# Two macaron blocks on one core: all 24 products of the modulation rows inside the FFNs, none in the transitions behind the norms

## Chip, cores and metric

One core of one Trainium2 chip runs the whole program. The metric is device time in microseconds (us) of one execution. Five engines run side by side, each with an instruction queue of its own: TensorE (PE; its weight loads are shown as PEld), VectorE (DVE), ScalarE (ACT), GpSimd (POOL) and SyncE (SP). Here SP does nothing but wait and issue the loads of weights. All arithmetic is float32.

## What is computed

There are two models in one program. The first, `first_block`, is a stack of DEPTH = 2 layers over 256 tokens of 1024 features:

```
for i in range(2):
    x = layer_norm(a*x + 0.5*swiglu(x, w1[i,0], w3[i,0], w2[i,0]))     # FFN 0, then norm 0
    x = layer_norm(a*x + token_mixing(x, w_in[i], ...))                # mix,   then norm 1
    x = layer_norm(a*x + 0.5*swiglu(x, w1[i,1], w3[i,1], w2[i,1]))     # FFN 1, then norm 2
    x = layer_norm(a*x + sigmoid(x @ ple_gate[i]) * (p[i] @ ple_proj[i]))  # ple, then norm 3
```

`swiglu` has a hidden width of 2816. The second model (attention, an FFN, an HGRN layer, an FFN) takes that output and a context of 256 tokens. Each of its layers is modulated: from a conditioning vector `c` (and a second one for the context) come six vectors of 1024 for each layer, `silu(c) @ ada_w[l] + ada_b[l]`, with `ada_w[l]` of 1024 x 6144. These are the modulation rows. They depend on `c` alone, so they can be computed at any time before the second model begins.

## The kernel before

**The modulation rows.** The two matrices `ada_w` are cut into 24 blocks of 1024 x 512 (2 MB each, `ADA_BLOCKS`). For each block there is a **product** and a **turn**. `pe_ada_product` (L2522) multiplies the block by `c_wide`, 8 k-tiles by 4 column groups, 32 matmul calls of 128 x 32 weights on 128 columns; the trace shows two instructions for each, 64 in all. ACT copies the bank to `ada_rows` (L2564). `pe_ada_turn` (L2542) transposes that one 128 x 128 tile on PE, and ACT copies 8 columns of it to `modp` (L2576). The blocks are taken in a fixed order, and nothing reads `modp` before `dve_parameters`, which runs in the down projection of the last FFN of layer 1.

**Where they stand.** Two tables say it. `IN_TRANSITION[l][n]` is the number of products in the transition behind norm n of layer l. `IN_FFN[i]` lists the blocks b (of 11) of the up projection in front of which one product is done in FFN i, in both layers; its turn comes in front of block b + 1 (`ffn_ada`, L2550). An assertion makes the sum 24. All engines and SP follow the same two tables.

**The FFN** (`pe_ffn7`, `act_ffn7`, `dve_ffn7`). The products with w1, w3 and w2 are done by a scheme with seven products of quarters in place of eight. In each of the 11 up blocks PE does seven groups of matmuls (112 instructions of 128 x 128 on 128 columns), DVE makes the sums of weight quarters for the next block (`dve_T`, L716), ACT copies four partial results out of PSUM (L670), DVE combines them (L756), and ACT ends a block with a SiLU (L688). Then come six down blocks in two halves. Two forms of the modulation product exist. In an FFN the block of `ada_w` has a place of its own in SBUF (`home`, the tile `f_ada`). SP issues that load from L405, in its queue right behind the loads of up block b, after waiting until ACT has emptied the bank of the product before it (`ada_used`):

```
if homes[0]:
    eng.wait_ge(ada_used, homes[0])
homes[0] += 1
eng.dma_start(f_ada[:], ...).then_inc(ada_landed, 16)
```

In a transition the block of `ada_w` goes through the ring of RING = 3 weight buffers (L359), in order with all other weights; a ring buffer is given back by the first matmul after its use.

**The transition** (`pe_transition` L1024 and below, `act_transition`) turns the normalized `xtok` (two tiles of 128 tokens) into `xT`. The order on PE is: eight transposes of tile 0 (L442), the first product if there is one, eight transposes of tile 1, then for two products: turn, second product, turn; and at the end a wait for DVE's last share of `xT`. On ACT:

```
act_ln_turn(act, l, n, 0, (0, 1), lambda: act_std(act, 1))
if products:
    act_ada_product(act)
act_ln_turn(act, l, n, 1, (0,))
```

`act_ln_turn` writes `xT` (L979), four instructions for each bank, `act_std` takes the square root of the variance for tile 1 (L963) between them, and DVE writes the last four pieces of `xT` (L999). The next stage starts on PE with transposes of parameter rows in the mix (L442 on `rows`), transposes of `p` in the ple (L442 on `xT`), or up block 0 of an FFN (L439).

Of the kernel before, what the change touches and what calls it, by code (L numbers as in the profile page):

```python
# [124 lines left out]
def two_blocks(nc, a, out):  # L125
    ctx = ExitStack()
    with ctx:
# [201 lines left out]
        def k_rows(w, c0, n):  # L329

            return w.rearrange("(k p) n -> p k n", p=P)[:, :, c0:c0 + n]
# [58 lines left out]
        def first_loads(eng, load, wide, ffn):  # L390
# [4 lines left out]
            def modulation(n):  # L395
                for _ in range(n):
                    l2, c0 = next(ada)
                    wide(a["ada_w_2"][l2], c0, 512)
# [8 lines left out]
            for l in range(DEPTH):  # L407
                ffn(a["ffn_w1"][l, 0], 0, a["ffn_w3"][l, 0], 0, a["ffn_w2"][l, 0], modulation_at_home, IN_FFN[0])
                modulation(IN_TRANSITION[l][0])
                wide(W[l], 1536, 288)  # L410
# [9 lines left out]
                wide(a["w_o"][l], 0, 1024)  # L420
                modulation(IN_TRANSITION[l][1])
                ffn(a["ffn_w1"][l, 1], 0, a["ffn_w3"][l, 1], 0, a["ffn_w2"][l, 1], modulation_at_home, IN_FFN[1])
                modulation(IN_TRANSITION[l][2])
                load((None, 0, k_rows(a["ple_w_proj"][l], 0, 1024)))
                wide(a["ple_w_gate"][l], 0, 1024)
                modulation(IN_TRANSITION[l][3])

# [40 lines left out]
        def pe_turn_x(pe, tts, banks):  # L468

            for tt, src in tts:  # L470
                pe.wait_ge(x_ready, pe.due(x_ready))
                for q in range(2):
                    pe.wait_ge(banks[q].freed, banks[q].next_free())
                    bank = banks[q].free_bank()
                    for k in range(4):
                        kt = 4 * q + k
                        mm = pe.turn(bank[:, k * P:(k + 1) * P], src[:, kt * P:(kt + 1) * P])
                        if k == 3:
                            mm.then_inc(banks[q].filled, 1)
# [480 lines left out]
        def act_std(act, n=2):  # L960
            for _ in range(n):
                act.wait_ge(var_ready, act.due(var_ready))
                act.e.activation(small[:, 3:4], small[:, 2:3], ACT.Sqrt).then_inc(std_ready, act.up(std_ready))  # L963
                act.wait_ge(std_ready, act.sent(std_ready))
# [7 lines left out]
        def act_ln_turn(act, l, n, tt, qs, between=None):  # L972

            for q in qs:
                act.wait_ge(to_act.filled, to_act.next_filled())
                bank = to_act.filled_bank()
                for k in range(4):
                    g, b = ln_gb(l, n, 4 * q + k)
                    ins = act.e.activation(xT[:, 4 * q + k, tt * P:(tt + 1) * P], bank[:, k * P:(k + 1) * P], ACT.Identity,  # L979
                                           scale=g, bias=b)  # L980
                    done = to_act.freed if k == 3 else act_step
                    ins.then_inc(done, act.up(done))
                    act.wait_ge(done, act.sent(done))
                    if between and q == 0 and k == 2:
                        between()
            act.sem_inc(x_turned, act.up(x_turned))
# [19 lines left out]
        def act_transition(act, l, n):  # L1006
# [3 lines left out]
            act_ln_turn(act, l, n, 0, (0, 1), lambda: act_std(act, 1))  # L1010
            products = IN_TRANSITION[l][n]
            if products:
# [11 lines left out]
        def pe_transition(pe, l, n):  # L1024

            pe_turn_x(pe, X2[:1], (to_act, to_act))
            products = IN_TRANSITION[l][n]
            if products:
# [1486 lines left out]
        ln_rows = at(arena_cols - 3 * P, P)  # L2515
        lb_rows = at(arena_cols - 3 * P, P)

        IN_TRANSITION = ((2, 0, 2, 0), (2, 0, 0, 0))
        IN_FFN = ((3, 5, 7, 8, 9), (3, 5, 7, 9))
        assert sum(sum(n) for n in IN_TRANSITION) + DEPTH * sum(len(m) for m in IN_FFN) == ADA_BLOCKS  # L2520

        def pe_ada_product(pe, home=False):  # L2522

            if home:
                pe.wait_ge(ada_landed, pe.due(ada_landed, 16))
                blk = f_ada
            else:
                blk = pe.block()
            pe.wait_ge(to_act.freed, to_act.next_free())
            bank = to_act.free_bank()  # L2530
            for k in range(KT):
                for j in range(4):
                    mm = pe.mm(bank[32 * j:32 * j + 32, 0:P], c_wide[:, k], blk[:, k, j * P:(j + 1) * P],
                               k == 0, k == KT - 1)
                    if k == j == 0 and not home:
                        pe.release(mm)
                    if k == KT - 1 and j == 3:
                        mm.then_inc(to_act.filled, 1)
            if not home:
                pe.used()  # L2540

        def pe_ada_turn(pe):  # L2542

            pe.wait_ge(ada_rows_ready, pe.due(ada_rows_ready))
            pe.wait_ge(to_act.freed, to_act.next_free())
            bank = to_act.free_bank()
            pe.turn(bank[:, 0:P], ada_rows[:, pe.ada % 2]).then_inc(to_act.filled, 1)
            pe.ada += 1

        def ffn_ada(marks, product, turn):  # L2550

            def between(b):
                if b - 1 in marks:
                    turn()
                if b in marks:
                    product()

            return between

        def act_ada_product(act, home=False):  # L2560

            act.wait_ge(to_act.filled, to_act.next_filled())
            bank = to_act.filled_bank()
            act.e.copy(ada_rows[:, act.ada_rows % 2], bank[:, 0:P]).then_inc(to_act.freed, act.up(to_act.freed))  # L2564
            act.wait_ge(to_act.freed, act.sent(to_act.freed))
            act.sem_inc(ada_rows_ready, act.up(ada_rows_ready))
            if home:
                act.sem_inc(ada_used, act.up(ada_used))
            act.ada_rows += 1

        def act_ada_turn(act):

            act.wait_ge(to_act.filled, to_act.next_filled())
            bank = to_act.filled_bank()
            n = act.ada
            ins = act.e.copy(modp[:, 8 * n:8 * n + 8].rearrange("p (j s) -> p j s", s=2),  # L2576
                             bank[:, 0:P].rearrange("p (j m) -> p j m", j=4)[:, :, 0:2])
            ins.then_inc(to_act.freed, act.up(to_act.freed))
            act.wait_ge(to_act.freed, act.sent(to_act.freed))
            act.ada += 1  # L2580
# [1072 lines left out]
        def first_pe(pe):  # L3653
            pe_turn_c(pe)
            pe_turn_x(pe, X2, (to_act, to_act))
            pe.wait_ge(c_cols_ready, pe.due(c_cols_ready))
            ada = [ffn_ada(marks, lambda: pe_ada_product(pe, True), lambda: pe_ada_turn(pe)) for marks in IN_FFN]
            for l in range(DEPTH):
# [13 lines left out]
        def first_act(act):  # L3672
            act_turn_c(act)
            act_turn_x(act, X2)
            act.sem_inc(ffn_x_ready, act.up(ffn_x_ready))
            ada = [ffn_ada(marks, lambda: act_ada_product(act, True), lambda: act_ada_turn(act)) for marks in IN_FFN]
            for l in range(DEPTH):
# [116 lines left out]
```

## Time and profile before

| | |
|---|---|
| median of 3 runs | 3774.65 us (3773.93 to 3776.23) |
| profiled execution: its own time | 3775.99 us |
| its span, first to last instruction | 3774.1 us |
| PE busy | 3379.8 us, 90% of the span |
| mean granted TensorE clock | 0.942 |
| loads of `ada_w` through L405 (FFNs) / L359 (ring) | 18 / 6, 2 MB each |

A time in the trace counts from the start of the span. "Busy" says that an instruction was under way. The granted clock is 1.00 at 2.4 GHz and 0.50 at 1.2 GHz; a value between them is a mean over a stretch with both levels.

### The profile page before, as it was taken

The page shows a single profiled execution, that of the slowest core. Times are in us where ns is not written, and L with a number is a line of the kernel's source. Part 1 is how long each engine was busy: PE and PEld are TensorE (multiplying, and loading weights), DVE is VectorE, ACT ScalarE, POOL GpSimd, SP SyncE. Part 2 cuts the span into 40 slices and gives each one's busy share as a digit, 9 for nine tenths or more (in the row PEclk, how much of TensorE's full clock was granted, in tenths as well). Part 3 has the DMA queues.
Part 4 walks back from the last instruction along what each step waited for, and adds up shares of the span by engine and source line. Part 5 has one row for each costly group of instructions (what it writes and reads, how often), then busy time and mean ns, then how long its engine had stood idle before and what let it go on. Part 6 is the DMA issues. An engine that isn't in the chain of part 4 may idle for free.

```text
span 3774.1 us, 44470 instructions
## 1 busy us (share of the span) xinstructions
PE 3379.8 (90%) x18658; PEld 2445.6 (65%) x18658; DVE 1791.2 (47%) x2674; ACT 637.4 (17%) x1204; POOL 37.9 (1%) x76
## 2 busy tenths in 40 slices
PE   8999978868998999987787997889999999998798
PEld 7986675465996997665554895445444444466597
DVE  5653355564655555255564664455210001268565
ACT  1111112101102102110220211144100001233110
POOL 1000000000000000000000000000000000000000
PEclk9999989888999999998898998989999999998899
DMA  7653301103745754400111653110222212221353
GB/s 256 221 200 113 123 1 67 67 1 106 261 153 195 256 177 155 165 26 23 67 45 45 221 202 128 48 67 1 67 67 67 84 61 73 104 97 45 108 166 112
DMA packets 273943, 419.24 MB, mean 111 GB/s; under 512 B 9784, under 2 KB 147360, under 8 KB 273616
## 3 DMA queue, kind: packets, MB, share of 16 engines
q1 hardware_dynamic: 268192, 399.98, 31.2%
q0 software_dynamic: 5088, 15.28, 1.2%
q8 instruction: 149, 2.44, 0.3%
q10 hardware_dynamic: 464, 1.12, 0.1%
q14 instruction: 50, 0.41, 0.0%
HBM read 415.32 MB, written 1.05 MB: 110 GB/s over the span
## 4 chain that ended last, share of the span: by engine, by line
PE 78%; DVE 16%; ACT 3%; issue 2%; DMA 0%; DVEq 0%; ACTq 0%; SPq 0%; PEldq 0%
PE bank L439 76%; PE bank L442 1%; DVE ctok L1682 1%; DVE arena L1671 1%; DVE arena L2244 1%; ACT xT L2655 1%; DVE arena L3081 1%; DVE arena L3454 1%; DVE arena L716 1%; DVE arena L3059 1%; DVE arena L3375 0%; DVE arena L3489 0%; DVE arena L1682 0%; DMA ring<-in_ffn_w 0%; ACT arena L2957 0%
## 5 line engine op out<-in xcount | busy, mean ns | idle before, releaser
L439 PE MATMUL bank<-xT,ring 128*128 128x128 f32 (+3 forms) x3872 | 888.1, 391 | 16.8 <-ACTq L2663 9.8
L439 PE MATMUL bank<-arena 128*128 128x128 f32 (+7 forms) x5428 | 745.1, 300 | 119.7 <-DVE arena L1565 14.5
L439 PEld LDWEIGHTS bank<-xT,ring 128*128 128x128 f32 (+1 forms) x3872 | 607.7, 193 | 294.5 <-issue 241.7
L439 PEld LDWEIGHTS bank<-arena 128*128 128x128 f32 (+3 forms) x5428 | 658.6, 185 | 187.0 <-DVEq L2008 15.3
L439 PE MATMUL bank<-ring,xT 128*128 128x512 f32 (+2 forms) x1408 | 566.8, 560 | 5.3 <-ACTq L1320 2.7
L439 PE MATMUL bank<-ring,arena 128*128 128x256 f32 (+1 forms) x1584 | 523.8, 487 | 22.6 <-ACTq L2473 11.5
L439 PEld LDWEIGHTS bank<-ring,xT 128*128 128x128 f32 x1408 | 262.5, 192 | 293.0 <-issue 285.0
L439 PEld LDWEIGHTS bank<-ring,arena 128*128 128x128 f32 x1584 | 305.6, 194 | 226.0 <-issue 176.8
L442 PE MATMUL bank<-cst,arena 128*128 128x128 f32 x610 | 106.9, 320 | 123.1 <-DVE arena L1627 15.1
L716 DVE TENSOR_TENSOR arena<-ring,arena 128x1024 f32<-128x1024 f32 (+1 forms) x170 | 202.9, 1193 | 5.9
L439 PE MATMUL bank<-arena,ring 128*128 128x128 f32 x1760 | 205.5, 275 | 0.0
L439 PEld LDWEIGHTS bank<-arena,ring 128*128 128x128 f32 x1760 | 201.0, 192 | 0.0
L756 DVE TENSOR_TENSOR arena<-arena,bank 128x256 f32<-128x256 f32 x165 | 69.5, 421 | 270.4 <-PE bank L439 168.6
L442 PEld LDWEIGHTS bank<-cst,arena 128*128 128x128 f32 x610 | 82.6, 164 | 159.0 <-issue 24.4
L670 ACT COPY arena<-bank 128x256 f32<-128x256 f32 x220 | 82.0, 373 | 562.9 <-PE bank L439 561.9
L856 DVE TENSOR_TENSOR arena<-bank,arena 128x512 f32<-128x512 f32 x22 | 15.2, 691 | 298.2 <-PE bank L439 298.2
L716 DVE TENSOR_TENSOR arena<-ring 128x1024 f32<-128x1024 f32 (+1 forms) x85 | 101.5, 1194 | 90.4 <-PE bank L439 67.6
L439 PE MATMUL bank<-xT,arena 128*128 128x128 f32 x880 | 107.2, 275 | 0.0
L716 DVE TENSOR_TENSOR ring<-ring 128x1024 f32<-128x1024 f32 (+1 forms) x85 | 101.5, 1194 | 2.9
L439 PEld LDWEIGHTS bank<-xT,arena 128*128 128x128 f32 x880 | 102.7, 192 | 0.0
L439 PE MATMUL bank<-ctok,arena 128*128 128x128 f32 x640 | 89.4, 294 | 14.4 <-DVE arena L1671 14.4
L2768 DVE TENSOR_TENSOR arena<-bank,lnp 128x512 f32<-128x512 f32 x20 | 13.8, 692 | 185.8 <-PE bank L439 185.8
(390 smaller groups left out, 2380.3 us busy)
## 6 DMA issues: line engine op xcount, KB each, us to landing
ring<-in_ffn_w SPq DMA_DIRECT2D x88, 1024.0 KB, 8.0
ring<-in_w_in SPq DMA_DIRECT2D x32, 2048.0 KB, 7.7
ring<-in_ffn_w_in SPq DMA_DIRECT2D x44, 1024.0 KB, 7.6
arena<-in_ada_w SPq DMA_DIRECT2D x18, 2048.0 KB, 13.8
ring<-in_ffn_w SPq DMA_DIRECT2D x16, 2048.0 KB, 7.8
ring<-in_hgrn_w_in SPq DMA_DIRECT2D x12, 2048.0 KB, 7.8
ring<-in_ffn_w_out SPq DMA_DIRECT2D x8, 2048.0 KB, 7.8
ring<-in_ffn_w SPq DMA_DIRECT2D x8, 1536.0 KB, 6.6
```

The costliest lines, as they stand in the source:

```text
L439: return self.e.matmul(o, lhsT, rhs, start=start, stop=stop, skip_group_check=True)
L442: return self.e.transpose(o, x, ident[0:n, 0:n])
L670: ins = e.copy(f_s[:, i], bank[:, 0:256])
L716: v.tensor_tensor(out_, a_, b_, ALU.subtract).then_inc(T_sums, dve.up(T_sums))
L756: ins = v.tensor_tensor(out_, kept, c, ALU.add)
L1671: v.tensor_tensor(Am[:, 4 * b:4 * b + 4], AT(b), lvlT[:, l:l + 1].broadcast_to([P, 4, P]), ALU.mult).then_inc(level_masked, dve.up(level_m ...
L1682: ins = v.tensor_tensor(X, bank[:].rearrange("p (h n) -> p h n", h=4), X, ALU.add)
L2244: v.reciprocal(dsq[:], dsq[:]).then_inc(dve_step, dve.up(dve_step))
L2655: ins = act.e.activation(xT[:, kt, s * SEQ:(s + 1) * SEQ], bank[:, j * SEQ:(j + 1) * SEQ], ACT.Identity, scale=Amod[:, l, which, kt, s:s + ...
L3059: ins = v.tensor_reduce(am[:, o + qt:o + qt + 1], bank[:], AX.X, ALU.max)
L3081: ins = v.tensor_scalar(pv, pv, r[:, qt:qt + 1], None, ALU.mult)
L3454: step(v.tensor_tensor(halves(dst, h, not back)[i], halves(src, h, not back)[i], halves(hF[back], h, not back)[i], ALU.mult))
```

## The change

The two tables are rewritten. The three pairs of products in transitions (behind norms 0 and 2 of layer 0 and behind norm 0 of layer 1) go. FFN 0 gains the mark 4 in both layers, FFN 1 the marks 4 and 8. The sum stays 24, the blocks keep their order, and each one from the seventh on is computed earlier or later by some places. SP's loads of these six blocks move with them, from L359 into the ring to L405 into `f_ada`.

```diff
-        IN_TRANSITION = ((2, 0, 2, 0), (2, 0, 0, 0))
-        IN_FFN = ((3, 5, 7, 8, 9), (3, 5, 7, 9))
+        IN_TRANSITION = ((0, 0, 0, 0), (0, 0, 0, 0))
+        IN_FFN = ((3, 4, 5, 7, 8, 9), (3, 4, 5, 7, 8, 9))
```

## Rows read from the trace of the kernel before

**Rows 1.** The page: the chain that ended last, and the loads through L405.

```profile
PE 78%; DVE 16%; ACT 3%; issue 2%; DMA 0%; DVEq 0%; ACTq 0%; SPq 0%; PEldq 0%
...
arena<-in_ada_w SPq DMA_DIRECT2D x18, 2048.0 KB, 13.8
```

**Rows 2.** Waits of PE, 1204 to 1413 us, FFN 0 of layer 1: total, times, longest.

```profile
PE bank L439 <- DVE arena L800: 0.4, 1, 0.4
```

**Rows 3.** Timeline of ACT, FFN 0 of layer 0, ends of blocks: start, duration in us.

```profile
49.08 0.63 ACT L688 ACTIVATE arena<-arena 128x512 f32<-128x512 f32 x1 [1.08 <-DVE arena L756]
61.58 0.63 ACT L688 ACTIVATE arena<-arena 128x512 f32<-128x512 f32 x1 [1.08 <-DVE arena L756]
...
130.57 0.63 ACT L688 ACTIVATE arena<-arena 128x512 f32<-128x512 f32 x1 [1.08 <-DVE arena L756]
...
145.27 0.63 ACT L688 ACTIVATE arena<-arena 128x512 f32<-128x512 f32 x1 [1.07 <-DVE arena L756]
```

**Rows 4.** Timeline there: a load of `ada_w`, and the product on PE that uses it.

```profile
117.06 0.37 SPq L405 DMA_DIRECT2D arena<-in_ada_w  x1
...
129.07 1.96 PE L439 MATMUL bank<-arena,cst 128*32 128x128 f32 x64
```

**Rows 5.** Loads of `ada_w` issued from 116 to 134 us (two): time to landing.

```profile
DMA to landing us min/median/max: 8.0/8.6/9.2
```

**Rows 6.** Timeline of PE, transition behind norm 0, layer 0, two products.

```profile
239.61 1.06 PE L442 MATMUL bank<-cst,xtok 128*128 128x128 f32 x8 [1.40 <-issue]
...
244.16 1.09 PE L442 MATMUL bank<-cst,xtok 128*128 128x128 f32 x8 [1.60 <-DVEq L888]
...
249.01 0.27 PE L442 MATMUL bank<-cst,rows 128*128 128x128 f32 x1
```

**Rows 7.** Timeline of PE, transition behind norm 2, layer 0, two products.

```profile
1139.59 1.06 PE L442 MATMUL bank<-cst,xtok 128*128 128x128 f32 x8 [1.39 <-issue]
...
1146.10 3.60 PE L439 MATMUL bank<-ring,cst 128*32 128x128 f32 x64
...
1150.36 0.60 PE L442 MATMUL bank<-cst,xT 128*128 128x128 f32 x4
```

**Rows 8.** Timeline of PE, transition behind norm 0, layer 1, two products.

```profile
1418.34 1.06 PE L442 MATMUL bank<-cst,xtok 128*128 128x128 f32 x8 [1.40 <-issue]
...
1427.46 0.27 PE L442 MATMUL bank<-cst,rows 128*128 128x128 f32 x1
```

**Rows 9.** Timeline of PE, transition behind norm 2, layer 1, no product.

```profile
2312.56 1.06 PE L442 MATMUL bank<-cst,xtok 128*128 128x128 f32 x8 [1.39 <-issue]
2317.10 1.97 PE L442 MATMUL bank<-cst,xtok 128*128 128x128 f32 x8 [3.48 <-DVEq L888]
2321.05 0.69 PE L442 MATMUL bank<-cst,xT 128*128 128x128 f32 x2 [1.98 <-DVEq L1004]
```

**Rows 10.** Windows at the three other transitions without products: stretch, length, busy by engine, granted clock, DMA.

```profile
917.40:927.60 10.20, 8.03 (x36) 7.66 (x37) 4.42 (x9) 3.49 (x8) 0.00 (x0) 0.50 0.40 128
...
1190.50:1204.10 13.60, 9.02 (x42) 8.25 (x41) 7.39 (x15) 6.07 (x14) 0.00 (x0) 0.50 0.30 93
...
2091.60:2098.40 6.80, 4.74 (x21) 4.38 (x22) 4.40 (x8) 3.01 (x7) 0.00 (x0) 0.50 0.09 17
```

**Rows 11.** Timeline of PE: the first matmul behind two of those transitions.

```profile
921.53 0.55 PE L439 MATMUL bank<-xT,ring 128*128 128x128 f32 x1 [2.04 <-DVEq L1004]
...
2095.62 0.55 PE L439 MATMUL bank<-xT,ring 128*128 128x128 f32 x1 [2.04 <-DVEq L1004]
```

**Rows 12.** Timeline of PE: start of the mix, and the ple, both of layer 0.

```profile
249.12 52.30 PE L439 MATMUL bank<-xT,ring 128*128 128x256 f32 x240
...
1158.71 27.63 PE L439 MATMUL bank<-ring,xT 128*128 128x512 f32 x64
```

**Rows 13.** Windows over the mix of layer 0 and of layer 1.

```profile
249.00:917.00 668.00, 558.58 (x2882) 405.27 (x2881) 334.03 (x543) 98.41 (x156) 3.71 (x7) 0.90 0.22 75
1427.40:2091.40 664.00, 553.78 (x2882) 401.51 (x2882) 334.59 (x543) 98.66 (x156) 3.70 (x7) 0.90 0.22 76
```

## Prediction

> **What bounds the kernel now.** I read the page first: 78% of the chain that ended last lies on PE, and no transfer has a share of it that shows [rows 1]. That is a mean over stages, so the stages that the change touches come next. In an FFN PE is the bound: in the waits of a whole FFN stretch PE waited once, for 0.4 us [rows 2]. In a transition PE is not: the timeline shows eight transposes, a pause until DVE has normalized the second tile, eight more transposes, and a pause until ACT and DVE have written `xT` [rows 6, 9]. So a piece of PE work costs its full length in an FFN and may cost nothing in a transition. Behind the transition PE is the bound again: 52.3 us of matmuls without a gap in the mix, 27.6 us in the ple [rows 12]. The third view is the granted clock in the windows. It shows that the transitions without products are stretches at 1.2 GHz [rows 10].
>
> **What six products more cost in the FFNs.** From the SiLU that ends one block to the next it is 61.58 - 49.08 = 12.50 us with nothing in between, and 145.27 - 130.57 = 14.70 us with the turn of one product and the next product in between [rows 3]. A product with its turn costs 2.20 us there, 1.96 us of it the 64 matmul instructions [rows 4]; nothing hides it. ACT's two small copies, the one wait on `ada_used` and the waits of PE are inside this difference, since the marks 7, 8, 9 of FFN 0 are already neighbours. Six more: 6 x 2.20 = +13.2 us.
>
> **The moved loads.** SP issues the `ada_w` load of a neighbouring mark once ACT has emptied the bank of the product before; queued behind it are the weights of a later block. That load is issued at 117.06 and its product starts at 129.07, 12.0 us later [rows 4]; it lands 8.0 and 9.2 us after its issue [rows 5]. Twelve products become neighbours of one before them (marks 4 and 5 in FFN 0, marks 4, 5, 8 and 9 in FFN 1, two layers) and have the same order of queue and the same margin of about 3 us. The ring loses six blocks of 2 MB at L359; what follows them (w_in, ple) is issued earlier. PE did not wait for a transfer there, so nothing is gained. I put the loads at 0.
>
> **What the transitions lose.** I measure each from the start of tile 0's transposes to PE's first instruction of the next stage. With products: 249.01 - 239.61 = 9.40 us [rows 6], 1150.36 - 1139.59 = 10.77 us [rows 7], 1427.46 - 1418.34 = 9.12 us [rows 8]. The same transition without products, behind norm 2 of layer 1, also follows an FFN: 2321.05 - 2312.56 = 8.49 us [rows 9]. The first product is hidden already: tile 1's transposes start 4.55 us after tile 0's with it [rows 6] and 4.54 us without [rows 9]. What goes is the tail: turn, second product, turn, with ACT's copies between. If all three become like the fourth, they give back 0.91 + 2.28 + 0.63 = 3.8 us. The 2.28 is large because the second product ran at half rate there, 3.60 us for the same 64 instructions [rows 7].
>
> **What the clock takes.** The 8.49 us already hold eight transposes at half rate, 1.97 us [rows 9] against 1.09 us [rows 6]. At the three other transitions without products the granted clock is 0.50 too, over 10.2, 13.6 and 6.8 us [rows 10]; so it fell at all four. With the products in place PE's pauses are 1.4 and 1.6 us long [rows 6], without them 3.48 and 1.98 us [rows 9]. I therefore take it that the clock falls at all three places where products go. It comes back some time after PE is dense again: in one case at 927.6, 6.1 us after the first matmul at 921.53, in another at 2098.4, 2.8 us after 2095.62 [rows 10, 11]. Dense matmuls at half rate lose half of that stretch, 3.0 or 1.4 us. The middle is 2.2 us, and since mix and ple are dense from their start [rows 12] I charge it in full three times: +6.7 us, with 4.2 and 9.2 as ends. Neither an edit of DVE's nor of ACT's own work is in the change; ACT loses two copies from each tail, off PE's path, at nothing.
>
> A rule speaks against the change as well. The Trainium skill ("TensorE: Matmul & The Clock Gate", Part 4: PE-mode transpose) says that transposes don't count as busy time of PE in the way that matmuls do; without products a transition holds transposes only. The trace agrees as far as it can: the clock was at its low level in all four of them. The same page (Terms) prices a low clock at the whole low time x one half. By it, with the mean of the three stretches, 10.2 us, the sum would be 13.2 - 6.5 + 3 x 5.1 = +22.0 us, or 3796.7; the rows say less, because PE stands idle in part of the low time.
>
> **The sum.** 13.2 - 3.8 + 6.7 = +16.1 us. The profiled execution took 3775.99 us (span 3774.1), so 3792.1 (span 3790.2); it stands 1.3 us above the median of the three runs, 3774.65, and by the median it is 3790.8. About 0.2%, 7.5 us, is what a measurement of this kernel can tell from no change.
>
> **Rivals.**
> 1. *The clock stays up* and the change is not slower. For it: the clock had just come through a dense FFN, and a short pause alone need not end it. Against it: the fourth transition has the same FFN before it and fell. Then the transposes take 1.09 us, not 1.97, the transitions give back 3.8 + 3 x (1.97 - 1.09) = 6.5 us, nothing is lost behind them, and the sum is 13.2 - 6.5 = +6.7 us: 3781.4, inside 0.2%. It decides only if it holds at all three places: one fall brings 0.9 + 2.2 us back, +9.8 in all.
> 2. *The product fits into a pause of PE's in the FFN* and costs nothing, if PE waits behind the product less than before. Against it: 14.70 us against 12.50, and 0.4 us of waits in all [rows 2, 3]. It would give -3.8 + 6.7 = +2.9 us: 3777.6.
> 3. *The `ada_w` loads come late.* The median of the 18 is 13.8 us to landing [rows 1], more than the 12.0 us that a neighbour has [rows 4]. If the twelve new neighbours landed like that, PE would wait 1.8 us at each: +21.6 us on top of 16.1, 3812. SP would be held with it and the weights of later blocks behind it. Against it: both neighbours in the view landed within 9.2 us, because they were issued ahead of the ring's loads and not behind them [rows 5]; the long ones stand behind ring loads.
> 4. *The program changes nothing of this* is no case: the tables drive all engines.
>
> **How the numbers follow.** The forecast has 0.80, rival 1 has 0.10, rival 2 has 0.03, rival 3 has 0.04. The rest, 0.03, is for a shift of the other stretches of low clock large enough to make it faster. That shift is the largest unknown besides: the mix of layer 0 and of layer 1 have the same 2882 matmul instructions and take 558.6 and 553.8 us of PE [rows 13], only because low stretches meet other work. When everything behind 62 us moves by a few us, they are dealt anew, and I allow 5 us either way. The forecast's own range is 13.2 - 3.8 + 4.2 - 5 = +8.6 to 13.2 - 3.8 + 9.2 + 5 = +23.6: 3783.3 to 3798.3. Widened to take in rival 1's middle, it is 3781 to 3799. Faster by over 0.2%: 0.03; within: 0.12 (rivals 1 and 2 in the main); slower: 0.85.
>
> **What the profile after will show.** Each step has its place. In all FFNs, six gaps of 14.6 to 14.7 us between SiLUs, five ordinary ones as before, PE without waits of more than 0.5 us. In the three transitions, no product, tile 1's transposes at 1.97 us rather than 1.09, first instruction of the next stage 8.5 us after tile 0's transposes, a granted clock of 0.50 from near the transposes until 3 to 6 us into the mix or ple. `ada_w` loads, 24 through L405 and none through L359, neighbours landing within 12 us. The forecast is wrong if the clock stays at 1.00 through two or all of these transitions, if PE waits at the marks, or if the clock in mix and second model deals out much more or less low time than before.

## The result: 15.1 us slower, and the profile after

The changed kernel takes 3789.75 us (median of 5 runs, 3789.01 to 3793.83), the kernel before 3774.65 us beside it (5 runs, 3773.93 to 3778.51). The ratio is 1.0040, 95% interval 1.0025 to 1.0055. That is +15.1 us, slower by clearly more than 0.2%. The forecast was 3790.8 us (+16.1), slower. The profiled execution took 3789.29 us, its span is 3787.5 us, 13.4 us more than the span before. Of all runs below only one, of the very last experiment, was far slower (5020.78 us, mean granted clock 0.667); its ratio and the median given there leave it out.

The timeline of PE shows the three transitions that lost their products; the lines stand against [rows 6], [rows 7] and [rows 8].

```profile
242.39 1.06 PE L442 MATMUL bank<-cst,xtok 128*128 128x128 f32 x8 [1.40 <-issue]
246.93 1.97 PE L442 MATMUL bank<-cst,xtok 128*128 128x128 f32 x8 [3.48 <-DVEq L888]
250.88 0.47 PE L442 MATMUL bank<-cst,rows 128*128 128x128 f32 x1 [1.98 <-DVEq L1004]
...
1143.95 1.06 PE L442 MATMUL bank<-cst,xtok 128*128 128x128 f32 x8 [1.39 <-issue]
...
1152.44 0.48 PE L442 MATMUL bank<-cst,xT 128*128 128x128 f32 x1 [1.98 <-DVEq L1004]
...
1424.87 1.06 PE L442 MATMUL bank<-cst,xtok 128*128 128x128 f32 x8 [1.39 <-issue]
...
1433.36 0.48 PE L442 MATMUL bank<-cst,rows 128*128 128x128 f32 x1 [1.98 <-DVEq L1004]
```

From the start of tile 0's transposes to the next stage it is 8.49 us in all three, as in [rows 9]. Tile 1's eight transposes take 1.97 us, half rate. The windows over the same places and behind norm 3 of layer 0 show the granted clock (the value behind POOL's):

```profile
244.90:255.10 10.20, 6.19 (x19) 4.98 (x20) 7.14 (x13) 4.32 (x10) 0.00 (x0) 0.50 0.16 45
1146.10:1159.70 13.60, 8.50 (x19) 4.61 (x20) 8.32 (x13) 5.52 (x13) 1.08 (x2) 0.50 0.15 46
1193.90:1207.50 13.60, 8.03 (x35) 7.26 (x36) 8.80 (x17) 6.13 (x15) 0.00 (x0) 0.50 0.14 44
1429.40:1436.20 6.80, 4.81 (x16) 3.87 (x17) 4.38 (x7) 3.00 (x7) 0.00 (x0) 0.50 0.08 6
```

Before, the first and the last of these places had the full clock and the second 3.4 us of the low one. The low stretch reaches 4.2, 7.3 and 2.8 us past the start of mix, ple and mix (255.10 - 250.88, 1159.70 - 1152.44, 1436.20 - 1433.36).

In the FFNs the ends of blocks on ACT stand against [rows 3]; the loads of `ada_w` and their landings against [rows 1, 5]:

```profile
62.17 0.63 ACT L688 ACTIVATE arena<-arena 128x512 f32<-128x512 f32 x1 [1.08 <-DVE arena L756]
76.75 0.63 ACT L688 ACTIVATE arena<-arena 128x512 f32<-128x512 f32 x1 [1.08 <-DVE arena L756]
91.45 0.63 ACT L688 ACTIVATE arena<-arena 128x512 f32<-128x512 f32 x1 [1.08 <-DVE arena L756]
```

```profile
L405 SPq DMA_DIRECT2D arena<-in_ada_w x24: 367/368/1772, 36.9 to 2218.9; - x24
...
DMA to landing us min/median/max: 7.8/9.1/13.9
```

The block with the first product takes 14.58 us, the one with a turn and the new product of mark 4 takes 14.70 us. All 24 loads go through L405, and the median landing is 9.1 us where it was 13.8 for the 18 of them before. Taken singly, the sixteen loads of marks that follow a mark directly landed in 7.8 to 9.2 us, the eight others in 12.5 to 13.9. PE's waits in FFN 1 of layer 0, over 921 to 1141 us, are as short as before the change; the first line is the end of the transition in front of it:

```profile
PE bank L439 <- DVEq L1004: 2.2, 1, 2.2
PE bank L439 <- DVE arena L800: 0.4, 1, 0.4
```

Where the 13.4 us of the two spans went, read from the starts of the same instructions in both timelines:

| stretch | before | after | difference |
|---|---|---|---|
| start, FFN 0 of layer 0 | 239.61 | 242.39 | +2.8 (0.6 of it before the first mark) |
| transition behind norm 0 | 9.40 | 8.49 | -0.9 |
| mix of layer 0, to tile 1's transposes of norm 1 | 668.51 | 666.51 | -2.0 |
| rest of norm 1, FFN 1 | 222.07 | 226.56 | +4.5 |
| transition behind norm 2 | 10.77 | 8.49 | -2.3 |
| ple | 39.67 | 42.82 | +3.2 |
| norm 3, FFN 0 of layer 1 | 228.31 | 229.61 | +1.3 |
| transition behind norm 0 | 9.12 | 8.49 | -0.6 |
| mix of layer 1 | 664.15 | 668.44 | +4.3 |
| rest of norm 1, FFN 1 | 220.95 | 225.33 | +4.4 |
| transition behind norm 2, all behind it | 1461.54 | 1460.37 | -1.2 |

### The profile page after: what moved, and what is told of

It reads as the page before. It is cut to its first block, busy times and chain, and to the rows that moved or that the text cites. A ratio compares the mean times of both kernels' runs of the same rounds, so it can differ in the third digit from the quotient of the medians.

```text
span 3787.5 us, 44484 instructions
## 1 busy us (share of the span) xinstructions
PE 3387.4 (89%) x18658; PEld 2452.1 (65%) x18658; DVE 1791.2 (47%) x2674; ACT 636.9 (17%) x1204; POOL 37.9 (1%) x76
## 4 chain that ended last, share of the span: by engine, by line
PE 78%; DVE 16%; ACT 3%; issue 2%; DMA 0%; DVEq 0%; ACTq 0%; SPq 0%; PEldq 0%
PE bank L439 77%; PE bank L442 2%; DVE ctok L1682 1%; DVE arena L1671 1%; DVE arena L2244 1%; ACT xT L2655 1%; DVE arena L3454 1%; DVE arena L3081 1%; DVE arena L716 1%; DVE arena L3059 0%; DMA ring<-in_ffn_w 0%; DVE arena L1682 0%; DVE arena L3375 0%; ACT arena L2957 0%; DVE arena L3489 0%
## 5 line engine op out<-in xcount | busy, mean ns | idle before, releaser
L439 PE MATMUL bank<-xT,ring 128*128 128x128 f32 (+3 forms) x3872 | 889.3, 391 | 17.5 <-ACTq L2663 10.2
L439 PEld LDWEIGHTS bank<-arena 128*128 128x128 f32 (+3 forms) x5428 | 665.0, 187 | 183.4 <-DVEq L2008 15.3
L442 PE MATMUL bank<-cst,arena 128*128 128x128 f32 x610 | 105.8, 317 | 120.2 <-DVE arena L1627 15.1
L439 PE MATMUL bank<-ctok,arena 128*128 128x128 f32 x640 | 89.6, 294 | 14.4 <-DVE arena L1671 14.4
L2768 DVE TENSOR_TENSOR arena<-bank,lnp 128x512 f32<-128x512 f32 x20 | 13.8, 692 | 185.9 <-PE bank L439 185.9
```

Of the source, the lines that this page charges most:

```text
L439: return self.e.matmul(o, lhsT, rhs, start=start, stop=stop, skip_group_check=True)
L442: return self.e.transpose(o, x, ident[0:n, 0:n])
```

## Experiments

All times are medians of repeated runs (5 or more of each), beside runs of the kernel before on the same chip: 3774.4 us for the first eight, 3774.5 for the last two. So wherever a run is set against the changed kernel (3789.75 us), the two were not measured side by side; the kernels before beside them agree within 0.3 us. In the runs that have one, a **filler** is a row of matmuls of the product's shape on constants, whose result nobody reads:

```diff
+        def pe_fill(pe, kt=KT):
+            pe.wait_ge(to_act.freed, to_act.next_free())
+            bank = to_act.banks[to_act.opened % 4]
+            for k in range(kt):
+                for j in range(4):
+                    pe.mm(bank[32 * j:32 * j + 32, 0:P], c_wide[:, k], inclU, k == 0, k == kt - 1)
```

### The FFN's half alone

The transitions keep their six products; the six more of the FFNs load and multiply six blocks a second time.

```diff
-            ada = iter([(n // 12, n % 12 * 512) for n in range(DEPTH * 6 * D // 512)])
+            ada = iter([(n % 24 // 12, n % 12 * 512) for n in range(30)])
...
-        IN_FFN = ((3, 5, 7, 8, 9), (3, 5, 7, 9))
+        IN_FFN = ((3, 4, 5, 7, 8, 9), (3, 4, 5, 7, 8, 9))
...
-            n = act.ada
+            n = act.ada % 24
```

> The kernel before with its transitions untouched and six more products in the FFNs, at the marks of the changed kernel (they compute blocks of ada_w a second time). Theory: 6 x 2.20 = +13.2 us on 3774.65, so 3787.9, and the transitions as before. Rival, loads that come late at neighbouring marks: up to 1.8 us more for each of twelve, 3800 and above. Rival, a product in an FFN is free: 3774.7.

3787.51 us (3785.46 to 3788.96), ratio 1.0031 (1.0020 to 1.0043): +13.1 us. The term was 6 x 2.20 = 13.2. The interval, +7.5 to +16.2 us, leaves out both the late loads and the free product. One thing did change in the transitions of its trace: the second product now runs at half rate behind norm 0 of layer 0 (3.51 us) and at full rate behind norm 2 (1.96 us), the other way round than before (1.95 and 3.60 us).

### The transitions' half alone

The FFNs keep their marks. The last six blocks of the modulation rows are left out, and ACT writes zeros in their place.

```diff
-        IN_TRANSITION = ((2, 0, 2, 0), (2, 0, 0, 0))
+        IN_TRANSITION = ((0, 0, 0, 0), (0, 0, 0, 0))
```

> The kernel before with the six products of the transitions left out altogether (six blocks of the modulation rows are never computed, zeros stand in their place); the FFNs have their nine marks a layer as before. Forecast's steps: -3.8 us of tails and +6.7 us of low clock behind them, +2.9: 3777.6. If the clock costs nothing (rival 1): -6.5, 3768.2. If only the tails count: -3.8, 3770.9.

3775.68 us (3774.01 to 3778.67), ratio 1.0003 (0.9994 to 1.0011): +1.3 us, not told apart from zero nor from the forecast's +2.9. The six products that leave the transitions, 64 instructions of PE each, give back nothing. A clock that costs nothing (-6.5 us) is out, and so is a gain of the tails alone (-3.8 us, 0.9990). The two halves add up to 13.1 + 1.3 = 14.4 us, against 15.1 for both.

### Filling the pauses of the changed kernel

The first filler stands between the tiles' transposes of the three transitions (64 instructions), the second behind tile 1's (48 instructions, `kt` = 6). The diff has both; each also runs alone.

```diff
             if products:
                 pe_ada_product(pe)
+            elif (l, n) in PAUSE:
+                pe_fill(pe)
             pe_turn_x(pe, X2[1:], (to_act, to_dve))
+            if (l, n) in TAIL:
+                pe_fill(pe, 6)
```

The first filler alone:

> The changed kernel with 64 matmul instructions of the product's shape, on constants and with a result that nobody reads, put back into the pause between the two tiles' transposes of the three transitions that lost their products. Clock theory: they cost nothing there, tile 1's transposes take 1.09 us again and not 1.97, the next stage starts 7.6 us after tile 0's transposes and not 8.5, and the low stretch behind it is gone: 3 x (0.9 + 2.2) = 9.3 us off the changed kernel's 3789.75, so about 3780.5, give or take 5 us for the low stretches elsewhere. Rival, the clock falls there whatever PE does in the pause: 3789.8 or up to 3 us more.

3787.01 us (3785.45 to 3789.59), ratio 1.0032 (1.0020 to 1.0044). That is 2.7 us below the changed kernel, not 9.3, and the intervals of the two ratios overlap. The timeline shows both a hit and a miss:

```profile
242.05 1.06 PE L442 MATMUL bank<-cst,xtok 128*128 128x128 f32 x8 [1.39 <-issue]
243.05 1.96 PE L439 MATMUL bank<-cst 128*32 128x128 f32 x64
246.59 1.09 PE L442 MATMUL bank<-cst,xtok 128*128 128x128 f32 x8 [1.59 <-DVEq L888]
249.67 0.48 PE L442 MATMUL bank<-cst,rows 128*128 128x128 f32 x1 [1.98 <-DVEq L1004]
```

The filler is hidden, tile 1's transposes take 1.09 us, the next stage starts 7.62 us after tile 0's transposes. That is 3 x 0.87 = 2.6 us, about the whole gain. But the first transpose of the next stage takes 0.48 us, half rate: the clock fell in the second pause instead of the first. The windows of this run at the start of mix, ple and mix:

```profile
249.40:252.80 3.40, 3.13 (x8) 2.38 (x9) 3.18 (x4) 0.46 (x1) 0.00 (x0) 0.50 0.15 14
1150.50:1157.30 6.80, 5.70 (x10) 2.72 (x11) 5.16 (x5) 1.74 (x4) 1.04 (x2) 0.50 0.18 44
1430.40:1433.80 3.40, 3.40 (x8) 2.59 (x9) 3.33 (x3) 0.11 (x1) 0.00 (x0) 0.50 0.22 30
```

Dense work had to run at half rate for 3 to 6 us nevertheless. My expectation, that the pause between the tiles decides, fell. Before, the second pause held the second product and the turns. From the end of the filler (245.0 us) to the next stage (249.67) PE now does eight transposes and nothing else for 4.7 us; whether the clock falls for the pause alone or also because only transposes stand ahead of it, no run here tells. Both fillers:

> The changed kernel with matmuls on constants, results unread, in both pauses of the three transitions that lost their products: 64 instructions between the tiles' transposes and 48 behind tile 1's, up to the wait for DVE's share of xT. Theory now: the products behind tile 1 kept the clock up for the next stage, the one between the tiles only for tile 1's transposes. So the next stage starts 7.6 us after tile 0's transposes with the clock at 1.00, and against the changed kernel 3 x 0.9 of the transposes and all of the 6.7 us behind come back: about 3780.5. Rival, the low stretch behind a transition comes whatever stands in the pauses: 3787, as with the first pause filled alone. Rival, 48 instructions are too long for the pause of 2 us: up to 0.5 us more each.

3783.27 us (3779.19 to 3788.19), ratio 1.0021 (1.0012 to 1.0030): 6.5 us below the changed kernel. The windows over the three transitions and what follows:

```profile
242.50:262.00 19.50, 17.31 (x181) 13.20 (x182) 15.74 (x24) 5.69 (x13) 2.62 (x5) 1.00 0.43 141
1144.30:1164.00 19.70, 16.84 (x157) 9.91 (x158) 10.38 (x16) 8.67 (x18) 1.08 (x2) 1.00 0.44 160
1420.70:1440.00 19.30, 17.13 (x180) 13.02 (x181) 15.56 (x24) 5.69 (x13) 2.61 (x5) 1.00 0.42 141
```

All three low stretches are gone. The median is 2.8 us above the expected 3780.5; its eleven runs spread over 9.0 us, so the size of the 6.7 us term is confirmed only to some 3 us by this pair. The profiled execution is even the slowest of the eleven, 3788.19 us, 1.1 us below the profiled one of the changed kernel: what it gained in the three transitions it lost elsewhere, for example to a low stretch from 359.6 to 366.4 us that the changed kernel's trace does not have. The second filler alone:

> The changed kernel with the 48 matmul instructions behind tile 1's transposes alone, the pause between the tiles left empty. Theory: the clock falls in the first pause as in the changed kernel, the 48 instructions run at half rate, 2.9 us, and end 0.9 us past DVE's share of xT (3 x 0.9 = +2.7 us), while denser work lets the clock return sooner, 1 to 2 us less dense work at half rate each (-2 to -3 us): 3789 to 3791. If the tail alone kept the clock: 3783.

3787.91 us (3780.22 to 3791.81), ratio 1.0031 (1.0019 to 1.0042). It lies 1.8 us below the changed kernel, which the spread of its six runs doesn't tell from nothing. The trace tells more. Its timeline, and the windows:

```profile
246.46 1.97 PE L442 MATMUL bank<-cst,xtok 128*128 128x128 f32 x8 [3.48 <-DVEq L888]
248.36 2.06 PE L439 MATMUL bank<-cst 128*32 128x128 f32 x48
250.41 0.33 PE L442 MATMUL bank<-cst,rows 128*128 128x128 f32 x1
```

```profile
246.10:249.50 3.40, 3.04 (x32) 2.63 (x36) 1.13 (x4) 3.08 (x8) 0.00 (x0) 0.50 0.02 5
249.50:262.00 12.50, 12.50 (x85) 9.16 (x78) 10.76 (x14) 0.23 (x1) 2.62 (x5) 1.00 0.65 216
```

Tile 1's transposes run at 1.97 us again and the fillers start at half rate, but the clock is back before the next stage starts, at 249.5 us against 250.41. It is so at the two other places (back at 1150.6 and 1427.1 us, next stages from 1150.75 and 1428.12).

These traces allow a comparison that the times are too coarse for. Each of the three places has the same work, from tile 0's transposes to a later group of matmuls in the next stage, with no other low stretch in between. The first two lines are that group in the mix of layer 0, before and after, the third is it in the ple after (before: 1158.71, [rows 12]):

```profile
301.35 2.96 PE L439 MATMUL bank<-arena,lnp 64*128 64x256 f32 x16
305.36 2.96 PE L439 MATMUL bank<-arena,lnp 64*128 64x256 f32 x16
1163.93 1.45 PE L439 MATMUL bank<-ring,xT 128*128 128x512 f32 x3
```

The distance from tile 0's transposes to these groups, in us:

| run | norm 0, mix of layer 0 | norm 2, ple | norm 0, mix of layer 1 | sum | against changed |
|---|---|---|---|---|---|
| before | 61.74 | 19.12 | 61.48 | 142.34 | -2.9 |
| changed | 62.97 | 19.98 | 62.24 | 145.19 | |
| transitions' half alone | 62.29 | 18.81 | 62.88 | 143.98 | -1.2 |
| first filler | 61.64 | 18.69 | 61.83 | 142.16 | -3.0 |
| second filler | 60.87 | 17.46 | 60.88 | 139.21 | -6.0 |
| both fillers | 60.30 | 15.97 | 60.30 | 136.57 | -8.6 |

So in the profiles the filler in the second pause gives back twice what the one in the first does, and it is the second pause that decides over the next stage. The times show less of it: the medians are 2.7, 1.8 and 6.5 us below the changed kernel, and low stretches elsewhere move single runs by more than that. For the second filler by itself the gain stands in its trace and not in its times.

### The transitions that never had a product

Nothing of the change is in these kernels. The first deals the six products of the transitions out one by one:

```diff
-        IN_TRANSITION = ((2, 0, 2, 0), (2, 0, 0, 0))
+        IN_TRANSITION = ((1, 1, 1, 1), (1, 1, 0, 0))
```

> The kernel before with its six products of transitions dealt out one to each of the transitions behind norms 0, 1, 2, 3 of layer 0 and 0, 1 of layer 1, all in the pause between the tiles; FFNs as before. Clock theory: the three tails go at full clock, 3 x about 2.1 = -6.5 us, and the three transitions that had no product gain 0.9 us in tile 1's transposes and 3.0, 3.0 and 1.4 us of low clock behind, -10.0: 3758.1. If the clock there falls in spite of a product: -6.5, 3768.2. If a product in the pause is not hidden: up to 2.2 us more for each of the three new places.

3782.62 us (3779.74 to 3786.28), ratio 1.0021 (1.0012 to 1.0030): 8.2 us slower, the wrong side of all three expectations. The timeline of DVE ahead of norm 1 of layer 0 names a wait that I had not looked for:

```profile
903.59 0.69 DVE L904 BATCH_NORM_STATS2 stats<-xtok 128x6 f32<-128x512 f32 x1
911.95 1.23 DVE L716 TENSOR_TENSOR arena<-ring 128x1024 f32<-128x1024 f32 x1 [7.67 <-DMA ring<-in_ffn_w]
```

Inside a norm that leads into an FFN, DVE makes the weight sums of up block 0 early (`dve_T`). A block of `ada_w` in the ring in front of that block pushes its load one buffer back. SP's issues show it, first of this run, then of the kernel before:

```profile
889.89 0.37 SPq L359 DMA_DIRECT2D ring<-in_ada_w  x1
903.63 20.29 SPq L359 DMA_DIRECT2D ring<-in_ffn_w  x4
```

```profile
887.51 35.82 SPq L359 DMA_DIRECT2D ring<-in_ffn_w  x6
```

The load of up block 0 is issued 16 us later, and DVE stands 7.7 us with the rest of the norm behind it; in the kernel before it did not wait there. The three places of this kind at such a price outweigh the clock. So the next run puts fillers there, which load nothing. It is the kernel before with both pauses filled behind norms 1 and 3 of layer 0 and norm 1 of layer 1:

> The kernel before, all products where they were, with both pauses filled in the three transitions that never had a product and lead into an FFN (behind norms 1 and 3 of layer 0, 1 of layer 1). Clock theory: tile 1's transposes at 1.09 us instead of 1.97 (3 x 0.9) and the low stretches behind them gone (3.0 + 3.0 + 1.4): -10.0 on 3774.4, so 3764.4, give or take 5 us. If fillers give only the transposes back: 3771.8. If the clock theory is wrong: 3774.4 or above.

**3763.79 us** (3761.86 to 3768.36), ratio 0.9971 (0.9960 to 0.9981): -10.6 us, the clock theory's number within 0.6 us. In the profiles the three stretches from such a transition to the norm behind its FFN, rows 4, 7 and 10 of the table of stretches above, are shorter by 3.4, 3.3 and 1.9 us (218.62, 225.02 and 219.09 us), 8.6 of the 10.0 expected; the rest of the match is low clock elsewhere, and luck. It is the best kernel of this study together with the next one, and it does 336 matmul instructions more than the kernel before. Its timeline at norm 1 of layer 0, and the windows behind two of its transitions, against [rows 10]:

```profile
911.73 1.04 PE L442 MATMUL bank<-cst,xtok 128*128 128x128 f32 x8
912.70 1.96 PE L439 MATMUL bank<-cst 128*32 128x128 f32 x64
915.33 1.09 PE L442 MATMUL bank<-cst,xtok 128*128 128x128 f32 x8 [0.68 <-DVEq L888]
916.35 1.52 PE L439 MATMUL bank<-cst 128*32 128x128 f32 x48
```

```profile
917.30:928.00 10.70, 9.75 (x106) 9.51 (x95) 8.80 (x12) 2.35 (x6) 0.00 (x0) 1.00 0.63 198
...
2088.00:2098.40 10.40, 9.45 (x100) 9.21 (x93) 8.51 (x11) 2.32 (x6) 0.00 (x0) 1.00 0.65 202
```

The last run of this kind fills the fourth transition too, and has four more fillers in PE's wait in the ple of layer 1:

> As the last one, with both pauses filled behind norm 2 of layer 1 as well and four times 64 instructions in the long wait of PE for p's transposes in the ple of layer 1. Clock theory: another 0.9 us of transposes and 2.2 us of the low stretch of 4.5 us that now lies on dense matmuls of the ple: 3761.3, give or take 5. Rival, DVE and ACT set the pace there: no more than the last one.

3763.46 us (3762.32 to 3765.96), ratio 0.9969 (0.9958 to 0.9981), no more than the last one, as the rival had it: PE waits for ACT there, 10.7 us without the four fillers. The stretch of 20 us at the low level is gone there, but the fillers end 4.0 us before ACT lets PE go on, and the clock falls in that rest and is low for the first 3.4 us of the ple:

```profile
2304.40:2324.20 19.80, 13.62 (x389) 12.27 (x390) 16.15 (x30) 6.88 (x17) 1.11 (x2) 1.00 0.15 55
2324.20:2327.60 3.40, 3.40 (x5) 1.35 (x4) 0.00 (x0) 0.27 (x1) 0.00 (x0) 0.50 0.21 34
```

### A shift and nothing else

The sum was off from the profiled pair by stretches that the change doesn't touch (the mixes: -2.0 and +4.3 us). Two runs are the kernel before with one filler (1.96 us) in front of up block 0 of the very first FFN, or with three in front of blocks 0, 1 and 2:

```diff
-                pe_ffn7(pe, ada[0])
+                if l == 0:
+                    pe_ffn7(pe, lambda b: (pe_fill(pe) if b in (0, 1, 2)[:1] else None, ada[0](b)))
+                else:
+                    pe_ffn7(pe, ada[0])
```

> The kernel before with 64 matmul instructions on constants, results unread, in front of up block 0 of FFN 0 in layer 0: everything behind moves by 1.96 us and nothing else changes. If the low stretches behind depend only on the work around them, the time is 3774.4 + 2.0 = 3776.3 and the trace shows the same low stretches 2 us later. If a shift deals them anew, single stretches appear, vanish or change length, and the time is off from 3776.3 by up to 5 us either way.

> The same in front of up blocks 0, 1 and 2: everything behind moves by 5.9 us. Without a new deal: 3780.3. With one: off from that by up to 5 us either way, and not by the same amount as the last one.

With 2 us more work, 3772.72 us (3772.40 to 3777.26), ratio 0.9999 (0.9990 to 1.0008), whose median is 3.8 us below 3774.54 + 1.96. The eleven runs fall into two heaps, seven at 3772.4 to 3774.0 and four at 3776.8 to 3777.3, and the interval of the ratio reaches to 3777.6, so the times alone don't settle it. With 6 us more (`[:3]` in place of `[:1]`), 3780.23 us in ten runs (3777.04 to 3784.28), ratio 1.0015 (1.0006 to 1.0024), 0.2 us below 3774.54 + 5.9. The traces show that low stretches are dealt anew. The timeline of PE at one place of the mix of layer 0, of the kernel before, of the changed kernel and of the 2 us shift, in this order:

```profile
355.21 4.83 PE L439 MATMUL bank<-ring,xT 128*128 128x8 f32 x32
```

```profile
359.22 3.74 PE L439 MATMUL bank<-ring,xT 128*128 128x8 f32 x32
```

```profile
357.73 3.74 PE L439 MATMUL bank<-ring,xT 128*128 128x8 f32 x32
```

The same 32 instructions of only 8 columns; the windows from 357.60 us, again of the kernel before and of the changed kernel, have the granted clock:

```profile
357.60:364.40 6.80, 6.80 (x24) 5.90 (x24) 0.00 (x0) 0.17 (x1) 0.00 (x0) 0.50 0.59 192
```

```profile
357.60:364.40 6.80, 6.80 (x47) 5.59 (x46) 0.00 (x0) 0.69 (x3) 0.00 (x0) 1.00 0.82 303
```

In the kernel before the clock falls in the middle of this narrow work and stays low for 6.8 us, up to 3.4 us of time. In the two others, where the same work starts 4.0 and 2.5 us later, it doesn't fall. With the shift of 6 us it falls there again (from 364.0 us).

That the shift does it is not shown. The kernel before and the one with fillers behind norms 1 and 3 have the same program up to norm 1 of layer 0, and start tile 0's transposes of norm 0 at 239.61 and 239.77 us. Yet the second, by its windows, is at the low level from 246.2 to 249.6 us and at the full one at 357.6, where the first is low. So one execution differs from the next by such stretches too, and one profile of each kernel can't tell the two causes apart.

## Why the prediction was right

**Six products in the FFNs, +13.2 us.** Right: +13.1 us with the transitions' products in place, and 14.70 us for a block at a new mark in the profile.

**Loads at 0, tails at -3.8 us.** Right: the neighbours' loads land in 7.8 to 9.2 us and no wait of PE for one shows; the transitions lose 0.91 + 2.28 + 0.63 = 3.8 us, to the hundredth what [rows 9] gave.

**The clock falls at all three places.** Right, and the low stretch reaches 4.2, 7.3 and 2.8 us past the start of the next stage, of which PE waits 0.7 us in the ple. From the first instruction of the next stage to the later group of the comparison above, PE needs 54.48, 11.49 and 53.75 us where it needed 52.34, 8.35 and 52.36: 2.1 + 3.1 + 1.4 = 6.7 us more, the term of the sum. With the tails' -3.8 that is the 2.9 us between the first two rows of the comparison. That the three come out at 2.2 us on average is in part luck: in the transitions' half alone the same three falls cost 1.5 + 2.0 + 2.0 = 5.5 us. That this is the clock and not the moved work rests on the fillers, which restore the clock, take work away from nobody and give 6.5 us back in the changed kernel (8.6 us in the comparison of the profiles) and 10.6 us in the kernel before. Which pause decides, the prediction left open; I took the one between the tiles at first, and that fell. The pause behind tile 1 decides over the next stage, the pause between the tiles over tile 1's transposes.

**What the sum did not hold.** 13.2 - 3.8 + 6.7 = 16.1, and the profiled pair shows 13.4. The 2.7 us are re-dealt low stretches: mix of layer 0 -2.0 - 2.1 = -4.1, mix of layer 1 +4.3 - 1.4 = +2.9, all behind the last norm 2 of layer 1 -1.2, norm 3 -0.9 (its low stretch ends after 4.1 us of dense work instead of 5.9), and +0.6 at the start and about +0.1 in the FFNs. The prediction allowed 5 us either way for it, and put it down to the shift of everything behind 62 us; that cause stays open, since executions of one program differ in the same way. The medians differ by 15.1, inside the same allowance; how they split over the low stretches the runs without a profile don't say.

**Rivals.** The clock that stays up is out by the windows, the free product by +13.1 us, the late loads by the landings. The Trainium skill's way to price the clock ("TensorE: Matmul & The Clock Gate", Terms: whole low time x one half) would take 0.5 x (10.2 + 13.6 + 6.8) = 15.3 us for the three places; the trace has 3 x 0.88 + 6.7 = 9.3 us, because PE is idle in part of it. The measured total is 6.9 us below the 22.0 us that it led to.

## What to carry to other kernels

A piece of TensorE work that stands in a pause of TensorE may be worth more than its own time: it can have the clock at 2.4 GHz for the dense stage behind. Before moving such work to a stage that TensorE bounds, price it there at full length (2.2 us each here), and price what the empty pauses do (0.9 us inside and 1.4 to 3.1 us behind each transition here). Where a transition must be short and PE has nothing to do, matmuls on constants that fill the pause right before the dense stage are a cheap remedy, and better in both pauses, -10.6 us of 3774 here for three transitions; real work there must not push the loads that another engine waits for early.

## What the runs showed of the hardware that I had not expected

- Filling the first of two pauses (3.5 us, cut to 1.6) did not keep the clock for the next stage; it fell in the second, of 1.98 us. With the second filled alone the clock fell in the first and was back before the next stage, in all three transitions of that trace. With both filled the next stage began at full clock in all seven transitions where it was tried; at one place, behind norm 3 of layer 0, the clock had fallen ahead of the first filler, which ran at half rate (3.09 us).
- A piece of work in the second pause can itself run low: the second product behind norm 2 of layer 0 took 3.60 us, and 3.51 us behind norm 0 in the run with six more.
- 2 us of extra work at the start did not make the program measurably longer (ratio 0.9999, 0.9990 to 1.0008, which doesn't leave out the 2 us either), and a low stretch of 6.8 us that begins in matmuls of 8 columns was gone from its trace, as it was from a trace without the shift. Differences of some 4 us between versions of this kernel say little of the edit unless the low stretches are compared.
- Runs of one kernel can fall into two heaps 4 to 5 us apart (3772.5 and 3777.1 with the 2 us shift).
